# Four landing slots for each expert table and batches of four pairs, with the next head's ranking in two places

## What is computed

```python
s1 = jnp.einsum('thd,hkd->thk', q[..., :half], p['peer_subkeys'][:, 0])
s2 = jnp.einsum('thd,hkd->thk', q[..., half:], p['peer_subkeys'][:, 1])
v1, i1 = lax.top_k(s1, PEER_TOPK)
v2, i2 = lax.top_k(s2, PEER_TOPK)
cand_s = (v1[..., :, None] + v2[..., None, :]).reshape(t, PEER_HEADS, PEER_TOPK * PEER_TOPK)
cand_i = (i1[..., :, None] * PEER_NKEYS + i2[..., None, :]).reshape(...)
best_s, pos = lax.top_k(cand_s, PEER_TOPK)
idx = jnp.take_along_axis(cand_i, pos, axis=-1)...
gate = jax.nn.softmax(best_s.astype(F32), axis=-1)...
def block(args):                       # 128 tokens at a time
    hb, ib, gb = args
    act = jax.nn.gelu(jnp.einsum('td,tkd->tk', hb, p['peer_u'][ib]))
    return jnp.einsum('tk,tkd->td', act * gb, p['peer_v'][ib])
```

## Time and profile before

| | us |
|---|---|
| median of three runs | 3908.39 |
| lowest and highest run | 3903.42, 3910.36 |
| span of the profiled execution | 3903.3 |

### The profile page before, as it was taken

How to read it: one execution, slowest core, us unless ns; L and a number is a source line. 1 busy time by engine, 2 the same in 40 slices (tenths; PEclk the granted TensorE clock), 3 DMA queues, 4 the chain that set the end, 5 groups by cost and what they waited for, 6 DMA issues and landing times. The chain is left out here.

```text
span 3903.3 us, 34180 instructions
## 1 busy us (share of the span) xinstructions
PE 3394.0 (87%) x11580; PEld 2105.4 (54%) x11580; DVE 1640.2 (42%) x3003; ACT 485.5 (12%) x951; POOL 892.9 (23%) x602
## 2 busy tenths in 40 slices
PE   6969999999999999899989998857776778667776
PEld 4545766757667576677778873333332333223332
DVE  6663443434434344211100002345556564656565
ACT  1111221212212122100000000011100101010100
POOL 0001201012010120001000000035555555545552
PEclk9779999999999999999999999878888889888888
DMA  6525455454554545443344453349999999999997
GB/s 253 194 99 207 164 184 195 146 222 160 188 193 148 222 157 191 155 133 128 110 156 146 151 224 140 108 178 424 425 424 425 424 425 424 425 424 424 424 424 319
DMA packets 148570, 972.20 MB, mean 249 GB/s; under 512 B 17081, under 2 KB 29722, under 8 KB 40570
## 3 DMA queue, kind: packets, MB, share of 16 engines
q0 software_dynamic: 73728, 536.90, 32.8%
q1 hardware_dynamic: 64474, 413.69, 29.2%
q10 hardware_dynamic: 10336, 21.21, 1.5%
HBM read 952.63 MB, written 19.10 MB: 249 GB/s over the span
## 5 line engine op out<-in xcount | busy, mean ns | idle before, releaser
L901 PE MATMUL ps<-mT,ring 128*128 128x256 f32 (+1 forms) x4096 | 1170.5, 446 | 2.1 <-PEq L212 2.1
L901 PEld LDWEIGHTS ps<-mT,ring 128*128 128x128 f32 x4096 | 775.8, 190 | 390.2 <-issue 320.4
L1807 PE MATMUL ps<-mT,diagonal 128*128 128x512 f32 x1024 | 484.9, 635 | 347.9 <-ACT diagonal L1617 346.5
L1807 PEld LDWEIGHTS ps<-mT,diagonal 128*128 128x128 f32 x1024 | 206.0, 204 | 626.7 <-issue 626.7
L1719 DVE CUSTOM_DVE_ANT_0 ring<-ring,h_rows 128x2048 f32<-128x2048 f32 x128 | 293.5, 2293 | 477.9 <-DMA ring<-in_peer_u_dram,expert_index 474.6
L1807 PE MATMUL ps<-v_rows,diagonal 128*128 128x512 f32 x1024 | 445.0, 592 | 1.2 <-DMA v_rows<-in_peer_v_dram,expert_index 1.2
L1807 PEld LDWEIGHTS ps<-v_rows,diagonal 128*128 128x128 f32 x1024 | 194.4, 190 | 246.8 <-issue 246.8
L1719 DVE CUSTOM_DVE_ANT_0 u_rows<-u_rows,h_rows 128x2048 f32<-128x2048 f32 x128 | 289.7, 2291 | 8.9 <-DMA u_rows<-in_peer_u_dram,expert_index 0.5
L1572 POOL DMA_INDIRECT ring<-in_peer_u_dram,expert_index x128 | 124.1, 970 | 700.6 <-issue 700.6
L1572 POOL DMA_INDIRECT v_rows<-in_peer_v_dram,expert_index x128 | 216.0, 1687 | 199.3 <-PE ps L1807 165.4
L670 POOL TENSOR_TENSOR rows<-rows,cT 128x2048 f32<-128x2048 f32 x16 | 72.1, 4527 | 775.4 <-ACT rows L738 775.4
(11 more groups left out here) (311 smaller groups left out, 2781.1 us busy)
## 6 DMA issues: line engine op xcount, KB each, us to landing
ring<-in_w_stream_dram SPq DMA_DIRECT2D x176, 1024.0 KB, 4.8
ada_tiles<-in_w_ada_dram SPq DMA_DIRECT2D x64, 1024.0 KB, 6.7
ring<-in_w_mix_dram SPq DMA_DIRECT2D x64, 768.0 KB, 4.3
rows<-cum_rows_scratch SPq DMA_DIRECT2D x16, 1536.0 KB, 13.7
ada_w_tiles<-in_w_scale_dram SPq DMA_DIRECT2D x16, 1024.0 KB, 6.0
ring<-in_w_out_dram SPq DMA_DIRECT2D x16, 1024.0 KB, 4.8
ring<-in_w_q_dram SPq DMA_DIRECT2D x16, 1024.0 KB, 4.7
hf_scratch<-hf ACTq DMA_DIRECT2D x8, 768.0 KB, 4.3
```

Of the source, the lines that this page charges most:

```text
L901: mm = nc.tensor.matmul(ps[:, k % 4, 0:n], m.ring[:, slot, kt * P:(kt + 1) * P], m.mT[:, kt, 0:n], start=(kt == 0), stop=(kt == KT - 1))
L1807: mm = nc.tensor.matmul(ps[:, 4 * t + b, :], dia[:, n, :], v_slot[n][:, b * 512:(b + 1) * 512], start=False, stop=False)
```

## The change

S becomes RING = 4 for both tables, and NB = TOPK // S = 4 batches make a unit, 64 in all. The slots in `u_rows` and `v_rows` are given up: U tiles land in the ring, V tiles in `mT`; `u_rows` is gone, and the tail's scratch rows `f` move to `v_rows`. All counts of the semaphores follow (`NB * i + h + 1`, `TOPK * i + S * h + n + 1`). The index buffer stays double, now taken by the batch's parity (`h % 2`). `select` is split into `rank_halves` and `rank_pairs`: the first stands behind the coefficients of a unit's first batch, the second behind those of the second batch, `weigh` behind those of the third, and ACT's exps for the next unit ahead of the third batch's gelu. The number of gathers, dots and products stays.

```diff
-        S = TOPK // 2
-        u_own = sb("u_rows", [P, S - RING, D])
+        S = RING
+        NB = TOPK // S
...
-        u_slot = [m.ring[:, n, :] if n < RING else u_own[:, n - RING, :] for n in range(S)]
-        v_slot = [mt[:, n, :] if n < RING else v_own[:, n - RING, :] for n in range(S)]
+        u_slot = [m.ring[:, n, :] for n in range(S)]
+        v_slot = [mt[:, n, :] for n in range(S)]
...
-                    for h in range(2):
-                        pool.wait_ge(idx_v, 2 * i + (h + 1))
+                    for h in range(NB):
+                        pool.wait_ge(idx_v, NB * i + (h + 1))
...
-                                pool.wait_ge(free, 2 * S * i + (S * h + n + 1))
+                                pool.wait_ge(free, TOPK * i + (S * h + n + 1))
...
-                                    slots[n], None, table, bass.IndirectOffsetOnAxis(ap=idx[:, h, n:n + 1], axis=0)).then_inc(into[n], 16)
+                                    slots[n], None, table, bass.IndirectOffsetOnAxis(ap=idx[:, h % 2, n:n + 1], axis=0)).then_inc(into[n], 16)
...
-                    for h in range(2):
-                        if h == 0:
+                    for h in range(NB):
+                        if h == 2:
 
                             act.wait_ge(arg_v, i + 2)
                             exps()
...
-                                    nc.vector.tensor_copy(idx[:, 1 - h, :], m.eidx[:, bass.ds(TOPK * i + (TOPK * HP * t + S * h + S), S)]).then_inc(idx_v, 1)
-                                if h == 0 and n == 3:
-                                    select(i + (HP * t + 1))
+                                    nc.vector.tensor_copy(idx[:, 1 - h % 2, :], m.eidx[:, bass.ds(TOPK * i + (TOPK * HP * t + S * h + S), S)]).then_inc(idx_v, 1)
...
                             if h == 0:
+                                rank_halves(i + (HP * t + 1))
+                            elif h == 1:
+                                rank_pairs(i + (HP * t + 1))
+                            elif h == 2:
                                 weigh(i + (HP * t + 1))
...
-                    h, f = m.h[:, t, :], u_own[:, t, :]
+                    h, f = m.h[:, t, :], v_own[:, t, :]
```

More of the change, by code:

```diff
@@ L1549, in _ @@
                 sp.dma_start(iota[:], d.iota).then_inc(small, 16)
-                sp.wait_ge(u_free, S + 2 * S * HP * TT)
+                sp.wait_ge(u_free, S + TOPK * HP * TT)
                 for n, (dst, src) in enumerate(((gt2, d.mod_rows[3 * KT:4 * KT]), (lng, d.ln[2]), (lnb, d.ln[3]))):
@@ L1577, in _ @@
                 nc.gpsimd.tensor_tensor(m.h[:, 0, :], m.h[:, 0, :], lng, ALU.mult).then_inc(turns, 1)
-                pool.wait_ge(turns, 4 * S * HP * TT + 1)
+                pool.wait_ge(turns, 2 * TOPK * HP * TT + 1)
                 nc.gpsimd.tensor_tensor(m.h[:, 0, :], m.h[:, 0, :], lnb, ALU.add).then_inc(out_p, 1)
@@ L1628, in _, with after, rank_halves @@
                 nc.vector.memset(m.sc[:, TT * 2 * PH:, :], 0.0).then_inc(zeroed, 1)
[L1630 to L1638, removed]
+                def after(n, k):
+                    v.wait_ge(sel, n)
+                    cs.inc(nc.vector.memset(idle[:, k:k + 1], 0.0))
+                def rank_halves(unit):
                     n = cs.inc(nc.vector.tensor_copy(scan[:], m.sc[:, span(2 * unit, 2), :]))
-                    after(n)
+                    after(n, 0)
                     for a in range(2):
                         n = cs.inc(nc.vector.max(best[:, a, 0:8], scan[:, a, :]))
-                    after(n)
+                    after(n, 1)
                     for a in range(2):
@@ L1647, in select @@
                         n = cs.inc(nc.vector.match_replace(scan2[:, a, :], best[:, a, 0:8], scan[:, a, :], -3.0e38))
-                    after(n)
+                    after(n, 2)
                     for a in range(2):
                         n = cs.inc(nc.vector.max(best[:, a, 8:16], scan2[:, a, :]))
-                    after(n)
+                    after(n, 3)
                     for a in range(2):
@@ L1654, in select, with rank_pairs @@
                     v.wait_ge(sel, n)
+                def rank_pairs(unit):
                     cs.inc(nc.vector.tensor_copy(bidxf[:], bidx[:]))
@@ L1659, in select @@
                                                        best[:, 1, :].unsqueeze(1).to_broadcast([P, TOPK, TOPK]), ALU.add))
-                    after(n)
+                    after(n, 4)
                     n = cs.inc(nc.vector.max(top[:, 0:8], cand[:]))
-                    after(n)
+                    after(n, 5)
                     cs.inc(nc.vector.max_index(pos[:, 0:8], top[:, 0:8], cand[:]))
                     n = cs.inc(nc.vector.match_replace(cand2[:], top[:, 0:8], cand[:], -3.0e38))
-                    after(n)
+                    after(n, 6)
                     n = cs.inc(nc.vector.max(top[:, 8:16], cand2[:]))
-                    after(n)
+                    after(n, 7)
                     n = cs.inc(nc.vector.max_index(pos[:, 8:16], top[:, 8:16], cand2[:]))
@@ L1704, in _ @@
                 v.wait_ge(sc_a, 1)
-                select(0)
+                rank_halves(0)
+                rank_pairs(0)
                 v.wait_ge(u_free, S)
@@ L1712, in _ @@
                         cs.enter(i, SELECT_STEPS)
-                        for h in range(2):
-                            step = 2 * i + (2 * HP * t + h)
+                        for h in range(NB):
+                            step = NB * i + (NB * HP * t + h)
                             v.wait_ge(gel_a, step)
@@ L1735, in _ @@
                 for t in range(TT):
-                    h, f = m.h[:, t, :], u_own[:, t, :]
+                    h, f = m.h[:, t, :], v_own[:, t, :]
                     v.wait_ge(ffn_pe, t + 1)
-                    v.wait_ge(u_free, S + 2 * S * HP * TT)
+                    v.wait_ge(u_free, S + TOPK * HP * TT)
                     for b in range(4):
```

6 lines of the change are left out of this document (3 added, 3 removed).

## The result

The changed kernel takes 3915.9 us (median of 20 runs, 3908.2 to 3919.6), the kernel before, run beside it, 3908.2 us (20 runs, 3898.7 to 3913.3). The ratio is 1.0018, with a 95% interval of 1.0012 to 1.0024: some 7 us slower (7.7 by the medians, 7.0 by the ratio). The forecast was 3907.4, one microsecond faster. The profiled execution has a span of 3913.5 us, against 3903.3 before.

A forecast was written before the change was run, and what follows sets the result against it. A full DMA queue, 424 GB/s of gathers, was taken to bound the expert stage. Stage 0 and tail -4.2 + 3.2 = -1.0 took the median from 3908.4 to 3907.4 us, range 3900.7 to 3920.

The forecast's parts named there:

- Stage 0: Expert stage: same gathers and bytes in a queue that never runs empty, so no time change, 0 us.
- wrong if the GB/s in the stage falls below 422: Expert stage: a stated test of failure, against a forecast of 424 GB/s in every stretch to about 3874.
- The last dot starts later than 3862: End of the expert stage: a stated test of failure, against a last U dot forecast at about 3858.9.
- the rivals: Dry queue at the fourth V slot, 0.14; GpSimd keeps the port, 0.12; no tail lock, 0.15; larger gain, 0.07.
- The slower rival: Expert stage: queue runs dry at the fourth V slot, 63 us (3970) or 16 us (3923); chance 0.14.
- The limit of T+22.9: Fourth V slot: latest issue of its next gather without a hole, T being when a batch's fourth U tile lands.
- The last dot starts as its tile lands: End of a batch's dots: taken as the start of the 3.57 us to the first matmul.
- TensorE's pieces: Expert stage: four pairs take 14.0 us at full clock, up to 17.0 after a cold restart, with idle to spare.
- The ranking: DVE: parts of 3.2 and 6.1 us, moved behind coefficients, fit in its 9 us idle, exact to 3 us for pairs.
- The tail: After the last U dot: tile 1 starts 4.2 us sooner, 3.2 lost beside GpSimd's steps, sum -1.0 us.
- GpSimd's lock: Tail: GpSimd's two steps on tile 0 hold up DVE's tile 1, 2.2 us at L1743 plus 1.0, sum 3.2.

The follow-up runs named there:

- e11: The kernel before with 128 bytes of padding ahead of ring and 384 ahead of `u_rows`, so all landing buffers start on a multiple of 256; 3898.7 us, ratio 0.9975.
- e2: The changed kernel with its four U slots in `u_rows` and four V slots in `v_rows` instead of ring and `mT`; 3901.5 us, one run.
- e9: The changed kernel with 128 bytes of padding ahead of the ring, so ring, `mT` and `v_rows` start on a multiple of 256; 3900.4 us, ratio 0.9974.
- e4: The kernel before with only the ranking split in two places and ACT's exps moved, slots and batches as before; 3906.1 us, one run.
- e12: The changed kernel with 64 bytes of padding ahead of the ring, buffers then 192 past a multiple of 256; 3915.1 us, ratio 1.0015.
- e5: The changed kernel with U's four slots in `u_rows`, V's still in `mT`; 3894.5 us, one run.
- e3: The kernel before with the two halves of each table's slots exchanged, `u_rows` and `v_rows` first; 3912.5 us, one run.
- e8: The changed kernel with only U's first slot in `u_rows`, the other three in the ring, V in `mT`; 3910.3 us, one run.

## Why the prediction was wrong

**The step that failed is "Stage 0"**, in its sentence "as long as the queue never runs empty, the last gather lands at 3874 us as now". It takes the time of the same bytes in a full queue as fixed. The condition was met (DMA share 1.01), the conclusion was not: 7.4 us. The 2.474 us per gather, was a mean of two paces. With about seven of every 16 gathers at 2.453 (e11's pace) and nine at 2.486 (the changed kernel's), the mean is (7 x 2.453 + 9 x 2.486) / 16 = 2.472. All 16 at 2.486 make 504 x (2.486 - 2.472) = 7.1 us more, which is the 7.4. The sign was there in the trace of before: dots 2.48 us apart in the ring and 2.43 in `u_rows`. The prediction's own measure "wrong if the GB/s in the stage falls below 422" is met over 2604 to 3851 (421), if only just: the slices of the page stand at 422. "The last dot starts later than 3862" is met clearly: 3870.21, which is 11.3 over the 3858.9 that were forecast, 3.9 of it from ahead of the stage and 7.4 from it.

None of the rivals was this one. The slower rival put the loss on the fourth V slot and a dry queue; e2 has the same four slots, the same waits and a quicker stage, and in the changed kernel the DMA share over the stage is 1.01 and the longest wait of DVE for a U tile is 9.9 us. So the queue was not dry there. The place that the rival named is real all the same: it is where e9 and e2 dip, in one batch of 64 and for 1.3 to 1.7 us, where the rival's prices were 16 and 63. The limit of T+22.9 fits all three kernels: T+22.7 cost nothing, T+23.9 and T+24.1 did.

One row was read wrongly without harm. "The last dot starts as its tile lands" does not hold for the dot of the earlier trace rows: it stands behind the ranking, in a run of dots 2.22 us apart, and its tile had landed before. The 3.57 us from that dot's start to the first matmul do hold for the changed kernel, where the fourth dot at 3174.20 is followed by the first matmul at 3177.78.

**The terms that held.** TensorE's pieces: the forecast was 14.0 to 17.0 us, with the clock at its low level at the start of a piece. The timeline has 15.69 us at 3873.78, the pieces that it shows whole in the stage take 15.45 to 17.07, and the stretches above show the restart from inside: 2.80 us of idle after which the granted clock is 0.50 (1.2 GHz) until 3181, then 1.00 (2.4 GHz). It cost the kernel no time, since a batch has 19.9 us and TensorE does not bound it. The Trainium skill, "TensorE: Matmul & The Clock Gate", section "HAM oscillation", says that a matmul loop which waits for its data at every tile starts each tile cold. The trace agrees: no whole piece is as short as the 14.0 us at full clock. The ranking: e4, 1244.7 against 1244.3.

**The tail**, -4.2 + 3.2 = -1.0, measured -1.1. By its parts: DVE starts tile 1 at 3892.99, 11.27 us behind tile 0's start, where the earlier trace rows had 3885.52 - 3860.23 = 25.29. At the same place of the gathers (last U dot) tile 0 begins 11.5 us behind the dot, 11.2 before, and tile 1 22.8 behind it, where before it was 36.5 - 9.9 = 26.6: 3.9 sooner for the 4.2. GpSimd's lock then takes 4.18 - 2.29 = 1.9 us at L1745 and 0.92 - 0.16 = 0.8 at L118, 2.7 in all for the 3.2. The terms were a little large each and their sum right. Which instruction is stretched followed: L1743, with one operand in PSUM, has its 2.48 us right beside GpSimd's step, L1745, with two in SBUF, lasts until just behind that step's end, and GpSimd's second step is in turn 6.43 long instead of 4.51. The Trainium skill, "SBUF — State Buffer", section "Who interferes with whom", says that a DVE instruction with two SBUF inputs contends with a GpSimd instruction that reads SBUF, and one with at most one does not. The trace agrees.

So the mechanisms that the prediction worked out were right, and the tail came out at -1.1. What it left out, the place where the rows land, was some seven times as large.

## What to carry to other kernels

Where a full DMA queue bounds a stage, the pace per transfer can depend on the place the rows land in, and a change of buffers is then a change of that pace. Cut the rate by buffer before calling it fixed: here a mean of 424 hid 428 and 421 at the same DMA share. Look up where the landing buffers start in the partition, and put them on a multiple of 256 bytes: for these gathers a pad of 128 bytes was worth some 15 us of 3916. Four slots and batches of four cost nothing in the changed kernel and some 1.6 us of the stage at the quicker pace, where a single gather came too late; look at short stretches, since the mean DMA share of 1.01 hid that as well.

## What the runs showed of the hardware

- Gathers of 128 rows of 8192 bytes take, by the starts of their packets, 2.453 us each with the destination on a multiple of 256 bytes (e11), 2.486 us at 128 bytes past it (after), and no more at 192 past (e12; 422 GB/s in both). DMA share shows nothing of it: 1.01 in each. The Trainium skill, "DMA: Bandwidth & Descriptors", section "How a descriptor splits into AXI transactions", says that the first transaction of a descriptor which doesn't start on a multiple of 256 bytes starts at the boundary below it, and it tells this of bytes that are read. Here it is the destination that is off the boundary. If the rule held for it too, a row of 8192 bytes would be 32 transactions or 33, an estimate of +3%; by the beats that the section counts, 260 at 128 past and 262 at 192 past against 256, an estimate of +1.6% and +2.3%. The runs have +1.3% at 128 past, near the beats, and the same at 192 past, which the beats don't give. So the runs have the same boundary and leave its price unexplained; they don't show the transactions.
- The quick pace outlasts the place: gathers into `mT` (before, e5), `v_rows` (e2) or the ring (e3, e8) behind gathers into `u_rows` stay quick for a few (428 GB/s in the kernel before from 3165.5 to 3182.5, where only four of seven gathers go to `u_rows`; two quick gathers in e8 with one slot). What carries it over wasn't found.
- Within e9 two slices of the page stand at 423 and 420 among 427 and 428. e2 has the same dips (423 and 418); e11 hasn't. The stretches above lie in these slices: around a single late gather the mean busy share of the DMA engines falls to 0.91 for a few microseconds. Why GpSimd starts it late is open, and so is the part of the dips that lies elsewhere.

```profile
GB/s 248 194 102 199 138 209 186 168 208 135 213 187 168 202 135 213 148 159 129 102 156 146 145 217 162 97 156 427 428 428 428 427 428 426 423 427 428 420 427 332
```
